# Dilated attention of a prompt: one joint maximum per query, transposed scores in a second pass, and no merge stage

## The chip, the cores and the metric

The kernel runs on one core of one Trainium2 chip. It is one launch: a 2,048-token prompt and 64 new tokens of eight samples go through one layer of a hybrid decoder. The metric is the device time of the launch in microseconds; lower is better.

## What is computed

The layer has three mixers side by side. The change concerns mixer B for the prompt, six heads of width 64, with three branches that share queries, keys and values: each query sees its own token and earlier ones at distance up to 128 (dilation 1), up to 512 (dilation 4), and up to 2,048 (dilation 16). Each branch is a softmax attention of its own; the branches are then merged with their softmax denominators:

```python
for window, dil in DILATIONS:            # ((128, 1), (512, 4), (2048, 16))
    s = einsum('bnirhe,bnjrhe->bnrhij', qs, kk) * scale    # blocks of 128 queries, 256 keys
    s = where(valid, s, -inf)
    mx = max(s, axis=-1);  p = exp(s - mx);  den = sum(p, axis=-1)
    outs.append(einsum('bnrhij,bnjrhe->bnirhe', p, vv) / den)
    lses.append(mx + log(den))
w = softmax(stack(lses), axis=0)
y_b = einsum('gbth,gbthe->bthe', w, stack(outs))
```

Taken together this is sum(p v) / sum(p) over all keys of all branches, with any common shift in the exponent. The projections before (`w_in`) and the output projection and the MLP behind are matrix products of the whole token set.

## The kernel before

The program is a chain of stages. Each has its own tiles and semaphores, and a barrier of all engines stands between two of them (`Mem.clear`, L70). Inside a stage every engine's instruction order is written out by hand, with semaphore waits between engines.

`project_phase` (L90) multiplies 17 tiles of 128 tokens by `w_in` in three passes over column ranges. TensorE (PE) does three matmuls per product; ScalarE (ACT) evicts each of the three column blocks of a tile (L295); SyncE (SP) stores them. `turns` lists the column groups that TensorE also transposes (L353), so that queries and keys lie with the head dimension on partitions in the scratch tensor `qkT`. In the third pass, which makes mixer B's queries, keys and values, only the last tile (the samples) is turned; the rows go to the scratch tensor `nat`.

`stick_prompt_phase` (L385) is mixer C. It matters here because it holds the matmuls that are nearest to the new ones: L584 does the scores of two heads with a 64-row contraction each, one in the upper and one in the lower half of the array.

`dilated_prompt_phase` (L628) handles 48 units: 16 blocks of 128 queries in each of the three branches. For one unit SP loads 128 rows of q, k and v of all heads from `nat` (L735). PE transposes q and k (L846), DVE (VectorE) and ACT copy them out (L791, L755), PE makes the scores of six heads with queries on partitions (L856). DVE adds the mask and takes the maximum in one instruction (L799), ACT takes the exponent with the row sum (L762), PE transposes the exponents (L825), DVE and ACT copy these (L781, L751), PE multiplies them with the values (L836), DVE evicts (L785), and GpSimd (POOL) stores output, maximum and sum to the scratch tensor `br` (L725).

`dilated_merge_phase` (L867) loads the three branches' rows for 128 tokens (L908), makes the weights on DVE in a row of small dependent instructions (L949 to L957), scales and adds (L958 to L961), transposes on PE (L977) and stores. The mLSTM stage follows, then the samples' stages, the output projection and the MLP.

## Time and profile before

| | |
|---|---|
| time, median of 3 runs | 4319.52 us (4317.83 to 4326.96) |
| the profiled execution | 4320.33 us, its span 4318.9 us |
| busy over the span | PE 3868.3 us (90%), DVE 1814.8 (42%), ACT 1410.2 (33%), POOL 1010.1 (23%) |
| projections | 0 to 704.8 us |
| mixer C, prompt | 704.8 to 1313.2 us |
| dilated attention, prompt | 1313.2 to 1675.3 us |
| merge | 1675.3 to 1783.3 us |
| all that follows | 1783.3 us to the end |

The stages don't overlap, because of the barriers. So the span is the sum of the stages, and each stage has its own bound: the busy shares over the whole span say nothing about one of them. The times of the stages are read where the first instruction of a stage starts. The busy time of PE is modelled for each matmul with its drain, so 100% doesn't mean that the array streams all the time.

### The profile page before, as it was taken

The numbers are of one execution on the slowest core, as the hardware profiler recorded it, in microseconds if no ns is written. First come the engines' busy times: TensorE is split into PE (matmuls) and PEld (weight loads), VectorE is DVE, ScalarE is ACT, GpSimd is POOL, SyncE is SP. The second block draws the span as 40 slices with busy tenths as digits, with TensorE's granted clock in tenths as the row PEclk, the third lists the DMA queues.
The fourth block names the chain that finished last, engine by engine and source line by source line (L and its number), as shares of the span: only waits on it lengthen the run. The fifth ranks groups of instructions, "written<-read, shape, count | busy, mean of one in ns | idle before, by whom it ended". The sixth has DMA issues, their size and how long they took to land. (4 is left out here: it accounts for less than half of the span.)

```text
span 4318.9 us, 62472 instructions
## 1 busy us (share of the span) xinstructions
PE 3868.3 (90%) x22579; PEld 3248.4 (75%) x22579; DVE 1814.8 (42%) x3743; ACT 1410.2 (33%) x3007; POOL 1010.1 (23%) x1192
## 2 busy tenths in 40 slices
PE   6999998999998984383669979799999999999998
PEld 6999996343437873383446658699999999999998
DVE  2211002555555666554236654443343443433533
ACT  2311113666664452120224532223223223222222
POOL 2111002444441000131124520051150240330310
PEclk9999998999999997555779989899999999999999
DMA  4654443010002333321939955545555546546433
GB/s 167 220 179 166 163 162 118 6 35 6 8 3 86 103 118 113 95 75 43 256 125 369 362 180 173 170 129 166 181 166 177 180 141 209 160 153 216 136 117 110
DMA packets 457305, 619.63 MB, mean 143 GB/s; under 512 B 43701, under 2 KB 352566, under 8 KB 454230
## 3 DMA queue, kind: packets, MB, share of 16 engines
q1 hardware_dynamic: 415406, 481.52, 35.2%
q0 software_dynamic: 24064, 75.82, 5.0%
q10 hardware_dynamic: 17578, 58.81, 4.1%
q8 instruction: 168, 2.75, 0.3%
q14 instruction: 89, 0.73, 0.1%
HBM read 508.96 MB, written 157.20 MB: 154 GB/s over the span
## 5 line engine op out<-in xcount | busy, mean ns | idle before, releaser
L3049 PE MATMUL p_PS<-p_HI,p_WUH 128*128 128x424 f32 (+1 forms) x1280 | 457.7, 358 | 16.1 <-DVE p_WUL L2985 16.1
L3051 PE MATMUL p_PS<-p_HI,p_WUL 128*128 128x424 f32 (+1 forms) x1280 | 455.0, 355 | 0.0
L3050 PE MATMUL p_PS<-p_LO,p_WUH 128*128 128x424 f32 (+1 forms) x1280 | 453.4, 354 | 0.0
L3050 PE MATMUL p_PS<-p_UL,p_WDH 128*128 128x424 f32 (+1 forms) x1280 | 452.9, 354 | 0.0
L3049 PE MATMUL p_PS<-p_UH,p_WDH 128*128 128x424 f32 (+1 forms) x1280 | 452.7, 354 | 0.0
L3051 PE MATMUL p_PS<-p_UH,p_WDL 128*128 128x424 f32 (+1 forms) x1280 | 452.4, 353 | 0.0
L374 PE MATMUL p_PP<-p_WH,p_HH 128*128 128x384 f32 (+1 forms) x1224 | 414.1, 338 | 27.3 <-DVE p_WL L305 27.3
L2995 DVE TENSOR_TENSOR p_WDL<-p_WD,p_WDH 128x512 fp32r<-128x512 f32 x320 | 221.2, 694 | 455.0 <-ACT p_WDH L2928 455.0
L375 PE MATMUL p_PP<-p_WL,p_HH 128*128 128x384 f32 (+1 forms) x1224 | 406.8, 332 | 0.0
L376 PE MATMUL p_PP<-p_WH,p_HL 128*128 128x384 f32 (+1 forms) x1224 | 406.5, 332 | 0.0
L2873 POOL CAST p_WUH<-p_WU 128x1024 fp32r<-128x1024 f32 x160 | 168.7, 1054 | 931.6 <-PE p_PS L3051 535.4
L2928 ACT ACTIVATE p_WDH<-p_WD 128x512 fp32r<-128x512 f32 x320 | 201.1, 631 | 488.2 <-PE p_PS L3051 480.4
L2985 DVE TENSOR_TENSOR p_WUL<-p_WU,p_WUH 128x1024 fp32r<-128x1024 f32 x160 | 211.4, 1323 | 325.9 <-POOL p_WUH L2873 325.9
L464 POOL TENSOR_TENSOR pc_SL<-pc_SL,pc_L 128x512 f32<-128x512 f32 (+3 forms) x216 | 232.1, 1090 | 200.8 <-DVE pc_L L548 200.8
L295 ACT ACTIVATE p_PT<-p_PP,p_rs 128x384 f32<-128x384 f32 (+1 forms) x153 | 87.2, 570 | 549.6 <-PE p_PP L376 549.6
L2919 ACT ACTIVATE p_R<-p_PS 128x424 f32<-128x424 f32 (+1 forms) x160 | 83.8, 524 | 547.3 <-PE p_PS L3051 547.3
L3049 PEld LDWEIGHTS p_PS<-p_HI,p_WUH 128*128 128x128 f32 x1280 | 241.2, 188 | 21.5 <-issue 16.5
L374 PEld LDWEIGHTS p_PP<-p_WH,p_HH 128*128 128x128 f32 x1224 | 231.5, 189 | 30.7 <-DVE p_WL L305 23.7
L3051 PEld LDWEIGHTS p_PS<-p_HI,p_WUL 128*128 128x128 f32 x1280 | 241.2, 188 | 7.5
L3050 PEld LDWEIGHTS p_PS<-p_LO,p_WUH 128*128 128x128 f32 x1280 | 241.4, 189 | 6.0
L3049 PEld LDWEIGHTS p_PS<-p_UH,p_WDH 128*128 128x128 f32 x1280 | 240.6, 188 | 5.2
L3051 PEld LDWEIGHTS p_PS<-p_UH,p_WDL 128*128 128x128 f32 x1280 | 240.5, 188 | 5.2
(427 smaller groups left out, 7223.6 us busy)
## 6 DMA issues: line engine op xcount, KB each, us to landing
p_WU<-in_w_up SPq DMA_DIRECT2D x160, 512.0 KB, 4.1
p_WD<-in_w_down SPq DMA_DIRECT2D x320, 256.0 KB, 2.7
sc_KP<-in_cache_sb_k SPq DMA_DIRECT2D x256, 192.0 KB, 5.3
sc_VP<-in_cache_sb_v POOLq DMA_DIRECT2D x256, 192.0 KB, 5.7
pb_X<-scratch_nat SPq DMA_DIRECT2D x48, 576.0 KB, 3.6
out_s_wk<-in_cache_win_k ACTq DMA_DIRECT2D x64, 382.5 KB
out_s_wv<-in_cache_win_v ACTq DMA_DIRECT2D x64, 382.5 KB
p_HH<-scratch_xh SPq DMA_DIRECT2D x34, 512.0 KB, 4.5
```

Of the source, the lines that this page charges most:

```text
L295: act.activation(PT[v % 2][:, a - o:e - o], PP[(3 * v + b) % 4][:, 0:e - a], ACT.Copy, scale=rs[:, t:t + 1]).then_inc(blk_ok, 1)
L374: pe.matmul(out, HH[s][:, k, :], wh, start=(k == 0), stop=False)
L375: pe.matmul(out, HH[s][:, k, :], wl, start=False, stop=False)
L376: ins = pe.matmul(out, HL[s][:, k, :], wh, start=False, stop=(k == KD - 1))
L464: ins = pool.tensor_tensor(new[:, a:CH], old[:, a:CH], L[u % 4][:, a:CH], ALU.add)
L2873: pool.tensor_copy(WUH[u % RU][:, :, :], WU[u % RU][:, :, :]).then_inc(wh_ok, 1)
L2928: act.activation(WDH[g % RS][:, :], WD[:, g % RD, :], ACT.Copy).then_inc(dh_ok, 1)
L2985: dve.tensor_tensor(WUL[u % RU][:, :, :], WU[u % RU][:, :, :], WUH[u % RU][:, :, :].bitcast(F32), ALU.subtract).then_inc(wl_ok, 1)
L2995: dve.tensor_tensor(WDL[g % RS][:, :], WD[:, g % RD, :], WDH[g % RS][:, :].bitcast(F32), ALU.subtract).then_inc(dl_ok, 1)
L3049: pe.matmul(out, hi, rhi, start=first, stop=False)
L3050: pe.matmul(out, hi, rlo, start=False, stop=False)
L3051: return pe.matmul(out, lo, rhi, start=False, stop=last)
```

## The change

Four things are changed.

1. In the third pass of the projections all 17 tiles are turned, not only the last. The stores of the same columns to `nat` are gone; the samples' stage reads its new values from the output tensor `s_wv` instead.
2. The dilated stage is rewritten, head by head. A pair is two units of one branch; a head has 24 pairs, six heads 144. A first pass (`natural` on PE, `maximum` on DVE) makes scores with queries on partitions and keeps only the row maxima. The maxima of the three branches are brought into one order through the scratch tensor `bm` (SP's `maxima` and `spread`), DVE's `joint` takes the largest, and SP loads it back, spread over all partitions (`MB`). A second pass (`scores`) makes the same scores again with keys on partitions; DVE subtracts the joint maximum of each query (`shifted`), ACT takes the exponent (`weights`), POOL zeroes what the band leaves out (`select`), and PE multiplies with a tile of 64 value columns and 64 columns of ones (`values`), so that 64 rows of the result hold the sum of the exponents. All branches accumulate in four PSUM banks; the third branch has another order of the tokens and is copied out first (`branch3`, `total`). The division is a logarithm and an exponent on ACT and a product on POOL. The first pass runs 36 pairs ahead of the second, the values three pairs behind it.
3. Queries, keys and values are loaded whole, one head at a time; both halves of the partitions hold the same head, so that the two units of a pair can use the two halves of the array.
4. The merge stage is gone.

In the code `b` is the branch, 0 for dilation 1, 1 for dilation 4, 2 for dilation 16; `u` is one of its 16 blocks. Tokens of branch 1 stand 16 bytes apart in `Q`, `K` and `MB`, tokens of branch 2 64 bytes.

```diff
@@ project_phase
-            return [(0, 0, 3, GB), (1, NB, 3, GB + 3)] if t == NT else []
+            return [(0, 0, 3, GB), (1, NB, 3, GB + 3)]
...
-                if p == 2:
-                    sp.dma_start(S["nat"][rows, QB:QC], part(QB, QC)).then_inc(p_out[s], 16)
@@ dilated_prompt_phase, whole body replaced
+    CY, NU, LEAD, LAG, NE = 24, 48, 36, 3, 6
+    TOTAL = HB * CY
+    TILE, HALF = SEQ // P, P // 2
+    def pair(j):
+        j = j % CY
+        if j < 8:
+            return 2, (2 * j, 2 * j + 1)
+        if j < 16:
+            n = (j - 8) // 2 * 4 + (j - 8) % 2
+            return 0, (n, n + 2)
+        return 1, (2 * (j - 16), 2 * (j - 16) + 1)
+    def ahead(a):
+        return pair(a + 8)
+    def width(b, u):
+        return P if b == 2 or u == TILE - 1 and b == 0 or b == 1 and u >= TILE - 4 else 2 * P
+    def earlier(b, u):
+        return b == 0 and u > 0 or b == 1 and u >= 4
+    def tokens(x, b, u, first, n):
+        if b == 0:
+            return x[:, (u + first) * P:(u + first + n) * P]
+        if b == 1:
+            lo = (u // 4 + first) * P
+            return x.rearrange("p (m f) -> p f m", f=4)[:, u % 4, lo:lo + n * P]
+        return x.rearrange("p (m f) -> p f m", f=16)[:, u, :]
...
+        MB = [m.sb(f"MB{i}", [P, SEQ]) for i in range(2)]
...
+        AC = [m.ps(f"AC{i}", [P, 512]) for i in range(4)]
+        ST = m.ps("ST", [P, 2, 512])
+        SA = m.ps("SA", [P, 2, 512])
...
+            def load_qk(h):
+                g, d, i = h // 2, slice(h % 2 * HD, (h % 2 + 1) * HD), h % 3
+                if h >= 3:
+                    sp.wait_ge(st_ok, upto(h - 3, CY - 1))
+                for dst, src in ((Q[i], S["qkT"][GB + g]), (K[i], S["qkT"][GB + 3 + g])):
+                    for a in range(2):
+                        sp.dma_start(dst[a * HD:(a + 1) * HD, :], src[d, 0:SEQ]).then_inc(qk_in[i], 16)
+            def load_v(h):
+                if h >= 2:
+                    sp.wait_ge(pv_ok, upto(h - 2, CY - 1))
+                v = O["p_wv"][:, h * HD:(h + 1) * HD]
+                for b, rows in ((2, v.rearrange("(i f) c -> i f c", f=16)), (0, v.rearrange("(n i) c -> i n c", i=P))):
+                    sp.dma_start(VV[h % 2][:, b * TILE:(b + 1) * TILE, h % 2, :], rows).then_inc(v_in[h % 2], 16)
+                for n in range(4):
+                    rows = v[n * 512:(n + 1) * 512, :].rearrange("(i f) c -> i f c", f=4)
+                    sp.dma_start(VV[h % 2][:, TILE + 4 * n:TILE + 4 * n + 4, h % 2, :], rows).then_inc(v_in[h % 2], 16)
+            def maxima(h):
+                s = h % 2
+                sp.wait_ge(mx_ok, 2 * upto(h, 15))
+                with nc.allow_non_contiguous_dma(reason="one maximum each"):
+                    sp.dma_start(S["bm"][h, 0, :].rearrange("(n i) -> i n", i=P), MX[s][:, 0, :]).then_inc(m_out[s], 16)
+                for n in range(4):
+                    sp.dma_start(S["bm"][h, 1, n * 512:(n + 1) * 512].rearrange("(i f) -> i f", f=4),
+                                 MX[s][:, 1, 4 * n:4 * n + 4]).then_inc(m_out[s], 16)
+                sp.wait_ge(m_out[s], 16 * 5 * (h // 2 + 1))
+                if h >= 2:
+                    sp.wait_ge(mj_ok, h - 1)
+                sp.dma_start(MR[s][:, :, :], S["bm"][h, 0:2, :].rearrange("b (p f) -> p b f", f=TILE)).then_inc(r_in[s], 16)
+            def spread(h):
+                s = h % 2
+                sp.wait_ge(mj_ok, h + 1)
+                sp.dma_start(S["bm"][h, 2, :].rearrange("(p f) -> p f", f=TILE), MJ[s][:, :]).then_inc(j_out[s], 16)
+                sp.wait_ge(j_out[s], 16 * (h // 2 + 1))
+                if h >= 2:
+                    sp.wait_ge(sub_ok, upto(h - 2, CY - 1))
+                sp.dma_start(MB[s][:, :], row_bcast(S["bm"][h, 2, :], P)).then_inc(mb_in[s], 16)
...
+            load_qk(0)
+            load_qk(1)
+            load_v(0)
+            load_qk(2)
+            load_v(1)
+            for h in range(HB):
+                if h >= 2:
+                    load_v(h)
+                maxima(h)
+                spread(h)
+                if h >= 1 and h + 2 < HB:
+                    load_qk(h + 2)
+                if h >= 2:
+                    store(h - 2)
+            store(HB - 2)
+            store(HB - 1)
...
+            def select(j):
+                b, us = pair(j)
+                x = EX[j % NE]
+                pool.wait_ge(e_ok, j + 1)
+                ins = pool.affine_select(out=x[:, :, 0:P], in_=x[:, :, 0:P], compare_op=ALU.is_ge, fill=0.0, base=0,
+                                         pattern=[[0, 2], [1, P]], channel_multiplier=-1)
+                n = sum(width(b, u) == 2 * P for u in us)
+                if n:
+                    ins = pool.affine_select(out=x[:, 0:n, P:], in_=x[:, 0:n, P:], compare_op=ALU.is_ge, fill=0.0, base=0,
+                                             pattern=[[0, n], [-1, P]], channel_multiplier=1)
+                ins.then_inc(sel_ok, 1)
+            def output(h, k, selected):
+                c = slice(k * 512, (k + 1) * 512)
+                pool.wait_ge(rd_ok, 4 * h + k + 1)
+                if h >= 2 and k == 0:
+                    pool.wait_ge(y_out[h % 2], 16 * (h // 2))
+                pool.wait_ge(sel_ok, selected)
+                pool.tensor_tensor(YT[h % 2][kept(h), c], FN[kept(h), c], RD[kept(h), c], ALU.mult).then_inc(y_ok, 1)
+                pool.wait_ge(y_ok, 4 * h + k + 1)
...
+            def inverse(h, k):
+                c = slice(k * 512, (k + 1) * 512)
+                act.wait_ge(fn_ok, 4 * h + k + 1)
+                if h:
+                    act.wait_ge(y_ok, 4 * (h - 1) + k + 1)
+                act.activation(RD[kept(h), c], FN[summed(h), c], ACT.Ln).then_inc(ln_ok, 1)
+                act.wait_ge(ln_ok, 4 * h + k + 1)
+                act.activation(RD[kept(h), c], RD[kept(h), c], ACT.Exp, scale=-1.0).then_inc(rd_ok, 1)
...
+            def maximum(a):
+                h, (b, us) = a // CY, ahead(a)
+                s = h % 2
+                if a % CY == 0 and h >= 2:
+                    dve.wait_ge(m_out[s], 16 * 5 * (h // 2))
+                dve.wait_ge(sa_ok, a + 1)
+                for i, u in enumerate(us):
+                    c = slice(0 if earlier(b, u) else P, 2 * P)
+                    dve.tensor_tensor_reduce(out=junk[i][:, c], in0=SA[:, i, c], in1=mask[:, c], scale=1.0, scalar=-3e38,
+                                             op0=ALU.add, op1=ALU.max, accum_out=MX[s][:, b, u:u + 1]).then_inc(mx_ok, 1)
+            def joint(h):
+                s = h % 2
+                dve.wait_ge(r_in[s], 16 * (h // 2 + 1))
+                dve.wait_ge(mx_ok, 2 * upto(h, CY - 1))
+                dve.tensor_tensor(MR[s][:, 0, :], MR[s][:, 0, :], MR[s][:, 1, :], ALU.max).then_inc(ja_ok, 1)
+                dve.wait_ge(ja_ok, h + 1)
+                if h >= 2:
+                    dve.wait_ge(j_out[s], 16 * (h // 2))
+                dve.tensor_tensor(MJ[s][:, :], MR[s][:, 0, :], MX[s][:, 2, :], ALU.max).then_inc(mj_ok, 1)
+            def shifted(j):
+                h, (b, us) = j // CY, pair(j)
+                x = EX[j % NE]
+                if j % CY == 0:
+                    dve.wait_ge(mb_in[h % 2], 16 * (h // 2 + 1))
+                dve.wait_ge(st_ok, j + 1)
+                if j >= NE:
+                    dve.wait_ge(pv_ok, j + 1 - NE)
+                w = [width(b, u) for u in us]
+                if w[0] == w[1]:
+                    ins = dve.tensor_tensor(x[:, :, 0:w[0]], ST[:, :, 0:w[0]], both(MB[h % 2], b, us, w[0]), ALU.subtract)
+                else:
+                    for i, u in enumerate(us):
+                        ins = dve.tensor_tensor(x[:, i, 0:w[i]], ST[:, i, 0:w[i]], tokens(MB[h % 2], b, u, 0, w[i] // P), ALU.subtract)
+                ins.then_inc(sub_ok, 1)
+            def total(h, k):
+                dve.wait_ge(pv_ok, upto(h, 17 + 2 * k))
+                dve.wait_ge(b3_ok, 4 * h + 4)
+                if h and k == 0:
+                    dve.wait_ge(y_ok, 4 * h)
+                dve.tensor_tensor(FN[:, k * 512:(k + 1) * 512].rearrange("p (i f) -> p i f", f=16),
+                                  AC[k][:, :].rearrange("p (i f) -> p i f", f=16),
+                                  B3[:, :].rearrange("p (f i) -> p i f", f=16)[:, 32 * k:32 * k + 32, :], ALU.add).then_inc(fn_ok, 1)
+            for a in range(LEAD):
+                maximum(a)
+                if a == CY + 4:
+                    joint(0)
+            for j in range(TOTAL):
+                if j + LEAD < TOTAL:
+                    maximum(j + LEAD)
+                shifted(j)
+                h, i = divmod(j, CY)
+                if i == CY - (LEAD - CY) and h + 1 < HB:
+                    joint(h + 1)
+                done = j - LAG - 2
+                if done >= 0 and done % CY in (17, 19, 21, 23):
+                    total(done // CY, (done % CY - 17) // 2)
...
+            def rows(i):
+                return slice(i * HALF, (i + 1) * HALF)
+            def natural(a):
+                h, (b, us) = a // CY, ahead(a)
+                if a % CY == 0:
+                    pe.wait_ge(qk_in[h % 3], 64 * (h // 3 + 1))
+                if a:
+                    pe.wait_ge(mx_ok, 2 * a)
+                for i, u in enumerate(us):
+                    n = 2 if earlier(b, u) else 1
+                    ins = pe.matmul(SA[:, i, (2 - n) * P:2 * P], tokens(Q[h % 3][rows(i), :], b, u, 0, 1),
+                                    tokens(K[h % 3][rows(i), :], b, u, 1 - n, n), start=True, stop=True)
+                ins.then_inc(sa_ok, 1)
+            def scores(j):
+                h, (b, us) = j // CY, pair(j)
+                if j:
+                    pe.wait_ge(sub_ok, j)
+                for i, u in enumerate(us):
+                    w = width(b, u)
+                    ins = pe.matmul(ST[:, i, 0:w], tokens(K[h % 3][rows(i), :], b, u, 0, 1),
+                                    tokens(Q[h % 3][rows(i), :], b, u, 0, w // P), start=True, stop=True)
+                ins.then_inc(st_ok, 1)
+            def values(j):
+                h, (b, us) = j // CY, pair(j)
+                if j % CY == 0:
+                    pe.wait_ge(v_in[h % 2], 16 * 6 * (h // 2 + 1))
+                if h and j % CY in (0, 2, 4, 6):
+                    pe.wait_ge(fn_ok, 4 * (h - 1) + j % CY // 2 + 1)
+                pe.wait_ge(sel_ok, j + 1)
+                for i, u in enumerate(us):
+                    for bank, lo, w in pieces(b, u):
+                        if b == 0:
+                            pe.wait_ge(b3_ok, 4 * h + bank + 1)
+                        ins = pe.matmul(column(AC[bank], b, u, bank, w), VV[h % 2][:, b * TILE + u, :, :].rearrange("p a e -> p (a e)"),
+                                        EX[j % NE][:, i, lo:lo + w], start=opened[(b == 2, bank)] == (b, u), stop=True, skip_group_check=True)
+                ins.then_inc(pv_ok, 1)
+            pe.wait_ge(ones_ok, 1)
+            for a in range(LEAD):
+                natural(a)
+            for j in range(TOTAL):
+                scores(j)
+                if j + LEAD < TOTAL:
+                    natural(j + LEAD)
+                if j >= LAG:
+                    values(j - LAG)
+            for j in range(TOTAL - LAG, TOTAL):
+                values(j)
@@ dilated_sample_phase
-            act.dma_start(VN[:, :, :], S["nat"][SEQ:SEQ + NS, VB:QC].rearrange("(b t) c -> t b c", t=DT)).then_inc(ok["new_in"], 16)
+            act.dma_start(VN[:, :, :], O["s_wv"][:, WIN - DT:WIN, :].rearrange("b t c -> t b c")).then_inc(ok["new_in"], 16)
@@ build
-        ("br", (3, SEQ, NB + 2 * HB)),
+        ("bm", (HB, 3, SEQ)),
...
-    dilated_merge_phase(nc, A, S, O)
```

On PE, in the dilated stage before, one unit of the first two branches (`pb_SP` holds scores, then turned exponents, then outputs; `pb_TP` the turned queries and keys):

```order
L856 MATMUL pb_SP<-pb_KT,pb_QT 128x128 x12
L836 MATMUL pb_SP<-pb_X,pb_PT 128x64 x12
L846 MATMUL pb_TP<-pb_ident,pb_X 128x128 x6
L822 ISA
L825 MATMUL pb_SP<-pb_ident,pb_PR 128x128 x4
L822 REGISTER_ALU
```

and after the change, two pairs in the middle of a head (`pb_ST` the scores of the second pass, `pb_SA` those of the first, `pb_AC` the accumulators):

```order
L1002 MATMUL pb_ST<-pb_Q,pb_K 128x256 x2
L992 MATMUL pb_SA<-pb_K,pb_Q 128x256 x2
L1017 MATMUL pb_AC<-pb_EX,pb_VV 128x256
L1017 MATMUL pb_AC<-pb_EX,pb_VV 128x128
L1002 MATMUL pb_ST<-pb_Q,pb_K 128x256 x2
```

Two more groups of four such transposes follow before. The transposes are gone from the stage; scores of a pair of units of one head alternate with the first-pass scores of the pair 36 further on.

On DVE, one unit before (the L799 pairs come three times):

```order
L785 COPY pb_OT<-pb_SP 128x384
L788 REGISTER_ALU
L791 COPY pb_KT<-pb_TP 64x384 x2
L780 ISA
L781 COPY pb_PT<-pb_SP 128x1024
L799 ISA pb_SM,pb_OT<-pb_SP,pb_mask 128x256
L799 ISA pb_OT 128x1
L799 ISA pb_SM,pb_OT<-pb_SP,pb_mask 128x256
```

and after:

```order
L923 ISA pb_junk,pb_MX<-pb_SA,pb_mask 128x256
L923 ISA pb_MX 128x1
L923 ISA pb_junk,pb_MX<-pb_SA,pb_mask 128x256
L923 ISA pb_MX 128x1
L946 TENSOR_TENSOR pb_EX<-pb_ST,pb_MB 128x512
L923 ISA pb_junk,pb_MX<-pb_SA,pb_mask 128x256
```

The copies are gone. In each pair DVE first takes two maxima (those of the pair 36 ahead) and then subtracts, and the next pair's maxima come behind that.

## Rows read from the trace of the kernel before

**Rows 1.** Stretches of stages (us, busy and instructions per engine, PEclk, DMA share, GB/s)

```profile
704.82:1313.24 608.42, 595.83 (x2064) 242.84 (x2064) 319.19 (x495) 384.87 (x721) 272.87 (x320) 0.99 0.06 21
1313.24:1675.30 362.06, 311.80 (x2538) 283.09 (x2538) 234.71 (x920) 171.55 (x673) 27.40 (x53) 0.97 0.32 106
1675.30:1783.26 107.96, 14.38 (x48) 8.05 (x48) 69.98 (x192) 3.49 (x17) 0.49 (x3) 0.50 0.45 119
```

**Rows 2.** Waits of the dilated stage: engine line, waited for, us, times, longest

```profile
ACT pb_PR L762 <- DVE pb_nm L805: 174.2, 49, 5.8
```

**Rows 3.** Timeline of ACT in the projections' second pass: start us, us

```profile
454.10 0.58 ACT L295 ACTIVATE p_PT<-p_PP,p_rs 128x384 f32<-128x384 f32 x1 [3.93 <-PE p_PP L376]
458.67 0.58 ACT L295 ACTIVATE p_PT<-p_PP,p_rs 128x384 f32<-128x384 f32 x1 [3.98 <-PE p_PP L376]
462.77 0.58 ACT L295 ACTIVATE p_PT<-p_PP,p_rs 128x384 f32<-128x384 f32 x1 [3.52 <-PE p_PP L376]
467.26 0.58 ACT L295 ACTIVATE p_PT<-p_PP,p_rs 128x384 f32<-128x384 f32 x1 [3.91 <-PE p_PP L376]
```

**Rows 4.** Timeline of mixer C: 64-row score matmuls of two heads, full clock

```profile
726.90 0.49 PE L584 MATMUL pc_ZP<-pc_QS,pc_K 64*128 64x128 f32 x4
727.32 0.71 PE L587 MATMUL pc_ZP<-pc_mask,pc_ident 128*128 128x128 f32 x4
...
731.77 0.70 PE L584 MATMUL pc_ZP<-pc_QS,pc_K 64*128 64x256 f32 x4
732.40 0.38 PE L587 MATMUL pc_ZP<-pc_mask,pc_ident 128*128 128x128 f32 x1
```

**Rows 5.** The same timeline, from a score matmul to the DVE instruction behind it

```profile
999.86 1.13 PE L584 MATMUL pc_ZP<-pc_QS,pc_K 64*128 64x512 f32 x4
...
1001.04 0.75 DVE L539 TENSOR_SCALAR pc_E<-pc_ZP,pc_bsb 128x512 f32<-128x512 f32 x1 [1.66 <-PE pc_ZP L584]
```

**Rows 6.** Timeline of the dilated stage: mask and maximum, 256 and 128 keys

```profile
1403.98 0.42 DVE L799 CUSTOM_DVE_ANT_0 pb_SM<-pb_SP,pb_mask 128x256 f32<-128x256 f32 x1 [1.74 <-PE pb_SP L856]
...
1404.33 0.42 DVE L799 CUSTOM_DVE_ANT_0 pb_SM<-pb_SP,pb_mask 128x256 f32<-128x256 f32 x1
...
1595.70 0.29 DVE L799 CUSTOM_DVE_ANT_0 pb_SM<-pb_SP,pb_mask 128x128 f32<-128x128 f32 x1 [2.23 <-POOLq L727]
...
1595.92 0.29 DVE L799 CUSTOM_DVE_ANT_0 pb_SM<-pb_SP,pb_mask 128x128 f32<-128x128 f32 x1
```

**Rows 7.** Groups by shape, mixer C: a DVE instruction on PSUM and SBUF

```profile
L548 DVE SCALAR_TENSOR_TENSOR pc_L<-pc_ZP,pc_bsb,pc_E 128x512 f32<-128x512 f32 x168 | 126.2, 751 | 94.9 <-ACT pc_E L493 94.9
```

**Rows 8.** Timeline of the dilated stage: from a DVE instruction to the waiting PE

```profile
1663.86 0.69 DVE L781 COPY pb_PT<-pb_SP 128x512 f32<-128x512 f32 x1 [1.10 <-PE pb_SP L825]
...
1664.70 0.29 PE L836 MATMUL pb_SP<-pb_X,pb_PT 128*128 128x64 f32 x1 [0.87 <-DVE pb_PT L781]
```

**Rows 9.** Timeline of PE in the dilated stage: twelve full-array matmuls of 128 columns

```profile
1400.82 2.84 PE L856 MATMUL pb_SP<-pb_KT,pb_QT 128*128 128x128 f32 x24
1403.49 0.33 PE L836 MATMUL pb_SP<-pb_X,pb_PT 128*128 128x64 f32 x2
```

**Rows 10.** Timeline of POOL in the dilated stage

```profile
1313.92 0.29 POOL L715 TENSOR_SCALAR_AFFINE_SELECT pb_ident<-pb_ident 128x128 f32<-128x128 f32 x1
```

**Rows 11.** Timeline of mixer C's start: first matmul, and two groups at the low clock

```profile
713.58 0.80 PE L584 MATMUL pc_ZP<-pc_QS,pc_K 64*128 64x128 f32 x4 [20.01 <-DMA pc_K<-scratch_qkT]
...
715.46 1.23 PE L584 MATMUL pc_ZP<-pc_QS,pc_K 64*128 64x256 f32 x4
```

**Rows 12.** Stretches (as Rows 1): third branch of the dilated stage, and the mLSTM stage

```profile
1630.00:1645.00 15.00, 12.37 (x95) 10.06 (x93) 10.29 (x54) 7.76 (x37) 1.08 (x2) 1.00 0.36 112
1800.00:1960.00 160.00, 140.04 (x658) 129.48 (x659) 83.76 (x262) 44.99 (x138) 46.51 (x75) 0.50 0.22 65
```

**Rows 13.** Groups by shape, mixer C: POOL and ACT on 512 columns

```profile
L464 POOL TENSOR_TENSOR pc_SL<-pc_SL,pc_L 128x512 f32<-128x512 f32 x144 | 179.9, 1271 | 200.8 <-DVE pc_L L548 200.8
...
L491 ACT ACTIVATE pc_E<-pc_E 128x512 f32<-128x512 f32 x168 | 104.4, 621 | 138.3 <-DVE pc_E L539 138.3
```

More of the change, by code:

```diff
@@ L149, in stores @@
         def stores(p, t):
-            a = [1, 2, 3][p]
-            return a + (2 * DB - 2 if p == 2 and t == NT else 0)
+            return 2 * DB if p == 2 and t == NT else [1, 2, 2][p]
         def stored(p, t):
@@ L663, in each @@
-    def each(eng, step):
-        for trips, first, prev, rows, before in bodies:
-            if trips == 1:
-                for q in range(4):
-                    step(first + q, q, prev[q], lambda v, q=q: rows(v, 0, q), prev[q - 1] if q else before)
-                continue
-            with eng.Fori(0, trips) as i:
-                for q in range(4):
-                    step(i * 4 + (first + q), q, prev[q], lambda v, q=q: rows(v, i, q), prev[q - 1] if q else before)
+    CY, NU, LEAD, LAG, NE = 24, 48, 36, 3, 6
@@ new lines, in pieces, with column @@
+    def pieces(b, u):
+        if b == 2:
+            return [(u // 4, 0, P)]
+        if b == 0:
+            if width(b, u) == P:
+                return [(u // 4, 0, P)]
+            return [(u // 4, 0, 2 * P)] if u % 4 < 3 else [(u // 4, 0, P), (u // 4 + 1, P, P)]
+        return [(u // 4 + i, i * P, P) for i in range(width(b, u) // P)]
+    def column(acc, b, u, bank, w):
+        if b == 2:
+            return acc[:, u % 4 * P:u % 4 * P + P]
+        if b == 1:
+            return acc.rearrange("p (m f) -> p f m", f=4)[:, u % 4, :]
+        lo = max(u * P - bank * 512, 0)
+        return acc[:, lo:lo + w]
@@ L729, in _ @@
-            each(pool, step)
-        @block.sync
-        def _(sp):
-            def step(u, q, prev, rows, before):
-                wait_apart(sp, pv_ok, u + 2, passed)
-                sp.dma_start(X[q][:, :, :, :].rearrange("p a g c -> p (a g c)"), rows(views)).then_inc(x_in[q], 16)
-            each(sp, step)
+            for h in range(2):
+                ins = pool.memset(VV[h][:, :, 1 - h, :], 1.0)
+            ins.then_inc(ones_ok, 1)
+            def select(j):
+                b, us = pair(j)
+                x = EX[j % NE]
[7 more added lines that the diff above has]
+                ins.then_inc(sel_ok, 1)
@@ L740, in _ @@
+            for k in range(4):
+                output(HB - 1, k, TOTAL)
         @block.scalar
@@ L829, in values @@
-            def values(u, q, prev):
-                n = 2 if prev else 1
-                pe.wait_ge(pa_ok, u + 1)
-                pe.wait_ge(pb_ok, u + 1)
-                for h in range(HB):
-                    for k in range(n):
-                        slot = (q - 1) % 4 if n == 2 and k == 0 else q
-                        ins = pe.matmul(SP[q % 2][:, 0, h * HD:(h + 1) * HD], PT[q % 2][:, h // 2, (h % 2) * n + k, :],
-                                        X[slot][:, 2, h // 2, h % 2 * HD:(h % 2 + 1) * HD], start=(k == 0), stop=(k == n - 1))
-                ins.then_inc(pv_ok, 1)
```

348 lines of the change are left out of this document (97 added, 251 removed).

## The prediction

> **What bounds the stages that change.** I read the stretches first. Barriers separate the stages, so only the edited ones matter: the dilated stage takes 362.1 us and the merge 108.0, 470.0 together; in the first PE is busy 86% at a granted clock of 0.97, in the merge only DVE has work, 70 of 108 us, and that in short dependent steps [rows 1]. The waits of the dilated stage show a loop from DVE's maxima over ACT to PE's transposes: ACT waited 174.2 us for the negated maximum [rows 2]. So before, PE is near its bound in one stage, and latency rules the other. The new stage has to be priced as a loop too, since each engine waits for another in every pair.
>
> **The projections.** 16 more tiles are turned, six transposes each. In the second pass, which turns the same way, the three column blocks of a tile end 4.57, 4.10 and 4.49 us apart, the 4.10 without a turn [rows 3]. A turn of six costs 13.16 - 3 x 4.10 = 0.86 us, on PE, which is the bound there. 16 x 0.86 = **+14 us**. The store to `nat` gives way to the smaller one to `qkT`, on a queue and DMA engines that PE doesn't wait for in this pass: nothing. The samples' new values come from another tensor in one load: nothing.
>
> **The new loop.** `ST` and `SA` are single tiles. PE may write `ST` for a pair only after DVE has subtracted the pair before; behind that on PE stand the first-pass scores into `SA`; DVE takes the two maxima of `SA` before it subtracts. So one pair costs, in a row: scores, first-pass scores, two maxima, subtraction, and two handovers. The value matmuls, ACT and POOL lie beside it.
>
> A full pair (2 x 256 columns in both passes):
> - scores: two 64-row matmuls in two halves of the array, start to the next group's start, 732.40 - 731.77 = 0.63 us [rows 4];
> - first-pass scores up to DVE's start: modelled end 0.70 [rows 4] plus 0.05 (999.86 + 1.13 to 1001.04) [rows 5]: 0.75;
> - two maxima, each 0.35 after the one before: 0.70 [rows 6];
> - subtraction, 512 elements, PSUM and SBUF in: 0.751 by the nearest instruction [rows 7], 0.69 by a plain eviction [rows 8]; I take 0.72;
> - DVE's end to PE's start, 1663.86 + 0.69 to 1664.70: 0.15 [rows 8].
>
> Sum **2.95 us**. A short pair (2 x 128): 0.42 + (0.49 + 0.05) [rows 4, 5] + 2 x 0.22 [rows 6] + 0.42 for 256 elements, as a maximum takes [rows 6] + 0.15 = **1.97 us**. A head has, counted from `width` and `earlier`, 14 full and 10 short pairs (one mixed pair counted as full) in either pass: 14 x 2.95 + 10 x 1.97 = 61.0, six heads **366 us**.
>
> What comes on top:
> - The first 36 maxima run alone, and so do the last 36 subtractions: 36 more handovers each way, 36 x 0.27 = 10 us.
> - The clock. After the loads PE starts at 1.2 GHz, where the same groups have modelled ends of 0.80 and 1.23 instead of 0.49 and 0.70 [rows 4, 11]: +0.31 short, +0.53 full. In the lead of 36 (24 full, 12 short) PE waits for DVE's maxima in every pair, so I keep it at the low clock: 24 x 0.53 + 12 x 0.31 = 16. The first 12 pairs of the loop, mostly short, likely too: 10 more. 26 us.
> - Second waits in front of instructions and the mixed pairs' split subtraction: estimate 4 us, from 0 to 12.
> - Start: 713.58 - 704.82 = 8.8 us from a stage's start to its first matmul behind a load of 2 MB [rows 1, 11]; head 0's queries and keys are 2 MB too: 9 us.
> - End: four inversions of two ACT steps, below 0.62 each, one product below 1.27 on POOL [rows 13], a store and the barrier: 13 us.
>
> Sum 366 + 10 + 26 + 4 + 9 + 13 = **428 us** for the 470 removed: **-42**. With the projections **-28 us**.
>
> What I cost at nothing, and its cover:
> - Value matmuls: 128 columns over the full array take (1403.49 - 1400.82)/12 = 0.22 [rows 9], a full pair's four 0.89 us. They have from the end of the first-pass scores to the next pair's start, 0.12 + 0.70 + 0.72 + 0.15 = 1.7 us. In the last 36 pairs the slack is 0.2 us.
> - POOL's zeroing: 0.29 for 128 elements [rows 10], so some 0.5 for 256, two per full pair: 1.0 of 2.95 us. If it takes over 0.87 each it becomes the bound of the last 36.
> - The trip of the maxima through memory (five stores, a load, a store, a spread load of 1 MB): for later heads nine pairs, some 20 us, lie between store and `joint`, and 12 more before the first subtraction. For head 0 the stores queue on SP's queue behind 9 MB of loads, 3 MB of these in pieces of 256 bytes. The maxima of its first 16 pairs are there after about 43 us, `joint` is reached at about 72, the lead ends at 89. I expect no wait; if the loads take over 60 us, each us beyond costs one.
>
> **Strided reads.** Two of the three branches read `Q`, `K` and `MB` with steps of 16 and 64 bytes, which no large operand does in this trace, so no row prices them; bounds are nothing and twice the streaming. I take nothing, since an fp32 matmul takes 1.7 ns per column [rows 9], which leaves a reader time. The Trainium skill says otherwise (SBUF — State Buffer, SBUF: two separate sides, in its note on cachelines): a read needs two hits in each 16-byte line for full rate. By it the sum gains rival 2's amount. No row here can show it.
>
> **Rivals.**
> 1. *The clock stays low.* The mLSTM stage has PE 88% busy by the modelled ends and still runs at 0.50 throughout, while the third branch of the old stage is 82% busy and stays at 1.00 [rows 12]. So neither level is safe from the busy share. In the new loop at the low clock a full pair is 4.01 us, and the scores and the values fill it without a gap, like nothing in the mLSTM stage; that speaks for a rise. If it never rises: 84 x 1.06 + 60 x 0.62 = 126 instead of the 26, and the value matmuls, 1.8 us, no longer fit: +8. Time 4292 + 108 = **4400 us**. If it only falls again in each head's short pairs, some 8 us a head: **4336 us**.
> 2. *Strided reads cost, and the kernel is slower.* In the 16 pairs of a head of branches 1 and 2, 10 are short and 6 full. If streaming doubles, both passes gain 2 x (6 x 0.43 + 10 x 0.21) = 9.4 us, the subtraction 6 x 0.5 + 10 x 0.25 = 5.5: 15 us a head, 89 us. Time **4381 us**. It decides from a third of that penalty on, since 28 us are to be lost.
> 3. *The clock is high throughout*, the lead too, because DVE and PE alternate quickly: 26 us less, **4266 us**. Against it: in the lead PE waits for DVE in every pair, and the stage starts at the low clock [rows 11].
>
> **How the numbers follow.** The sum goes against the profiled execution, 4320.3 us, 0.8 above the median of the runs: 4320.3 - 28 = **4292 us**. Chances: forecast 0.47 (its own range 4276 to 4310), rival 3 0.10, clock falling in short pairs 0.11, strided reads 0.20 (4335 to 4390), clock low throughout 0.12. The range 4262 to 4388 takes in all but the last of these. A measurement of this kernel can tell some 0.2%, 9 us, from no change. Faster by more: 0.60; within: 0.08; slower: 0.32.
>
> **What the new profile would show.** The dilated stage starts 14 us later than 1313.2 and lasts 428; full pairs 2.9 to 3.0 us apart on the subtraction's line, short ones 2.0; DVE idle about 1.4 us per full pair, waiting for PE; the clock 0.5 for the first 100 us and 1.0 then; no wait of DVE for a load beyond a few us. I am wrong if a pair of branch 1 takes longer than one of branch 0 (strides), if POOL's selects end the values' wait and PE's scores are behind them, or if the last 36 pairs, priced at 1.8 us full, take over 2.

## The result, and the profile after

| | before | after |
|---|---|---|
| median of the runs | 4324.69 us (15 runs) | 4331.26 us (4328.24 to 4336.68, 15 runs) |
| ratio to before | | 1.0017, 95% interval 1.0009 to 1.0024 |
| span of the profiled execution | 4318.9 us | 4330.7 us |

The changed kernel is slower by 0.17%. The interval doesn't take in a ratio of 1, but the difference lies inside the 0.2% that I called "no change"; I had forecast 28 us less. So 35 us are to be explained. (The two profiled executions lie 11.8 us apart, the medians 6.6; the stages below add up to the former.) The four stretches of the profile after, by the first instruction of each stage (columns: window, its length, busy time of each engine with its count of instructions, the granted clock of PE, share of the DMA engines, GB/s):

```profile
0.00:715.33 715.33, 672.29 (x4080) 665.61 (x4080) 108.00 (x160) 130.88 (x240) 75.27 (x32) 0.99 0.49 163
715.33:1323.06 607.73, 595.17 (x2064) 242.62 (x2064) 319.00 (x495) 384.89 (x721) 272.79 (x320) 0.99 0.06 21
1323.06:1794.01 470.95, 373.36 (x1908) 252.47 (x1908) 216.69 (x762) 120.48 (x223) 124.36 (x257) 0.81 0.32 68
1794.01:4330.70 2536.69, 2286.44 (x13945) 2059.42 (x13945) 1099.66 (x2008) 719.36 (x1357) 633.47 (x785) 0.92 0.55 172
```

Against [rows 1], the projections are 10.5 us longer, mixer C is 0.7 shorter, and all that follows is 1.1 longer. The new dilated stage lasts 471.0 us, where I had forecast 428. It replaces 470.0 us and gains nothing. The same view splits it into the lead (up to the first subtraction), the loop of 108 pairs with both passes, and the last 36 pairs:

```profile
1323.06:1405.67 82.61, 41.40 (x152) 20.02 (x152) 25.47 (x151) 1.28 (x1) 6.05 (x5) 0.50 0.62 128
1405.67:1713.90 308.23, 264.43 (x1401) 187.24 (x1402) 155.04 (x566) 87.20 (x164) 81.91 (x181) 0.85 0.29 61
1713.90:1781.03 67.13, 64.71 (x333) 42.58 (x334) 32.59 (x45) 26.55 (x50) 30.93 (x67) 1.00 0.12 32
```

The end, 1781.03 to 1794.01, is 13.0 us. By my own terms these four would be 77, 286, 52 and 13 us; how each comes out stands in the section on the prediction. The excess is 22 us in the loop, 15 in the last pairs and 5 in the lead.

The timeline shows one full pair of branch 0 and one of branch 1, both at clock 1.0 and both with the same number of columns in the two passes (start, duration, engine, line, operation). In each, L946 is the subtraction of one pair and, at the end, that of the next; between them stand L1002, the scores of the next pair, L992, the first-pass scores, and L923, the first of the two maxima:

```profile
1509.51 0.69 DVE L946 TENSOR_TENSOR pb_EX<-pb_ST,pb_MB 128x512 f32<-128x512 f32 x1
...
1510.25 0.70 PE L1002 MATMUL pb_ST<-pb_Q,pb_K 64*128 64x256 f32 x4 [0.42 <-DVE pb_EX L946]
...
1510.79 0.60 PE L992 MATMUL pb_SA<-pb_K,pb_Q 64*128 64x256 f32 x4
...
1511.43 0.42 DVE L923 CUSTOM_DVE_ANT_0 pb_junk<-pb_SA,pb_mask 128x256 f32<-128x256 f32 x1 [1.24 <-PE pb_SA L992]
...
1512.12 0.69 DVE L946 TENSOR_TENSOR pb_EX<-pb_ST,pb_MB 128x512 f32<-128x512 f32 x1
```

```profile
1521.43 1.05 DVE L946 TENSOR_TENSOR pb_EX<-pb_ST,pb_MB 128x512 f32<-128x512 f32 x1
...
1522.53 1.28 PE L1002 MATMUL pb_ST<-pb_Q,pb_K 64*128 64x256 f32 x4 [0.78 <-DVE pb_EX L946]
...
1523.63 0.61 PE L992 MATMUL pb_SA<-pb_K,pb_Q 64*128 64x256 f32 x4
...
1524.29 0.42 DVE L923 CUSTOM_DVE_ANT_0 pb_junk<-pb_SA,pb_mask 128x256 f32<-128x256 f32 x1 [1.82 <-PE pb_SA L992]
...
1524.98 1.04 DVE L946 TENSOR_TENSOR pb_EX<-pb_ST,pb_MB 128x512 f32<-128x512 f32 x1
```

In branch 1, where MB, Q and K are read with a step of 16 bytes, the subtraction takes 1.05 us instead of 0.69 and the scores 1.28 instead of 0.70. The first-pass scores of that pair belong to branch 0 (the passes are 36 pairs apart) and cost no more. From subtraction to subtraction that is 3.55 us; in branch 0 it is 2.61 here, and 2.62 in nearly all pairs of the loop that are full and of branch 0 in both passes. This is the sign I had named for rival 2, the strided reads.

At the low clock the strides cost the matrix engine next to nothing. Two full pairs of the lead, of branch 0 and of branch 1:

```profile
1343.98 1.23 PE L992 MATMUL pb_SA<-pb_K,pb_Q 64*128 64x256 f32 x4 [0.88 <-DVE pb_MX L923]
```

```profile
1361.78 1.28 PE L992 MATMUL pb_SA<-pb_K,pb_Q 64*128 64x256 f32 x4 [0.88 <-DVE pb_MX L923]
```

So in the loop the strides took away what the high clock gives. The view by windows of two equal steps with strides in both passes (second pass of branch 2, first pass of branch 1), one at the high clock and one at the low, has the same length for both, 3.09 us:

```profile
1551.22:1554.31 3.09, 2.36 (x12) 1.50 (x12) 2.27 (x7) 0.42 (x1) 0.41 (x1) 1.00 0.80 242
1620.89:1623.98 3.09, 2.87 (x14) 1.92 (x13) 2.27 (x9) 0.42 (x1) 0.41 (x1) 0.50 0.64 202
```

### The profile page after: what moved, and what is told of

It reads as the page before. It is cut to its first block and busy times, and to the rows that moved or that the text cites. A ratio compares the mean times of both kernels' runs of the same rounds, so it can differ in the third digit from the quotient of the medians.

```text
span 4330.7 us, 59154 instructions
## 1 busy us (share of the span) xinstructions
PE 3927.3 (91%) x21997; PEld 3220.1 (74%) x21997; DVE 1743.3 (40%) x3425; ACT 1355.6 (31%) x2541; POOL 1105.9 (26%) x1394
```

## The experiments

Each is an edit of the changed kernel unless it says otherwise. e1, e2, e3, e5, e10 and e11 leave out the dilation of branches 1 and 2 in the operands named, so these branches attend to wrong tokens or subtract wrong maxima; they price the strides and are no kernels to use. The others leave nothing out. Times are medians; the ratio is to the kernel before, run beside it, with its 95% interval.

| label | edit | us | ratio (interval) |
|---|---|---|---|
| e1_contiguous | Q, K, MB read in blocks | 4270.6 | 0.9882 (0.9863 to 0.9902) |
| e2_contiguous_mb | MB alone | 4309.9 | 0.9974 (0.9965 to 0.9984) |
| e3_contiguous_qk | Q and K alone | 4284.8 | 0.9913 (0.9895 to 0.9931) |
| e5_contiguous_stationary | the stationary operand alone | 4319.0 | 0.9996 (0.9987 to 1.0005) |
| e6_before_turned | before, with the turned tiles | 4333.2 | 1.0024 (1.0014 to 1.0033) |
| e4_subtract_first | DVE subtracts first | 4285.6 | 0.9921 (0.9904 to 0.9938) |
| e7_maxima_before_values | e4, maxima stored first | 4271.5 | 0.9883 (0.9868 to 0.9899) |
| e9_maxima_first_alone | maxima stored first, alone | 4330.0 | 1.0012 (1.0003 to 1.0022) |
| e10_contiguous_maxima_first | e1, maxima stored first | 4250.3 | 0.9828 (0.9812 to 0.9844) |
| e11_contiguous_both_orders | e10 with e4 | 4213.3 | 0.9746 (0.9730 to 0.9763) |
| e8_three_orders_of_maximum | e7, MB in three orders | 4342.6 | 1.0049 (1.0034 to 1.0065) |
| e12_lead_30 | e7, lead of 30 pairs | 4256.8 | 0.9838 (0.9821 to 0.9856) |

### Strides taken away: e1, e2, e3, e5

```diff
-            return x.rearrange("p (m f) -> p f m", f=4)[:, u % 4, lo:lo + n * P]
-        return x.rearrange("p (m f) -> p f m", f=16)[:, u, :]
+            return x.rearrange("p (f m) -> p f m", f=4)[:, u % 4, lo:lo + n * P]
+        return x.rearrange("p (f m) -> p f m", f=16)[:, u, :]
```

This is `tokens` (Q and K, e3); the same in `both` (MB) is e2, and e1 has the two. e5 has it only where `tokens` gives the stationary operand.

> The changed kernel, but branches 1 and 2 read Q, K and MB in contiguous blocks of 128 or 256 columns in place of every 4th or 16th element; numbers, shapes and order of the instructions are the same. So these two branches attend to wrong tokens: the kernel leaves out the dilation. Theory (the strides are what the new stage lost): in the loop a pair of branch 1 takes 3.56 us and one of branch 0 2.62 with the same columns. With contiguous reads both should take 2.6, a short pair beside a full one 2.15 in place of 3.09, short beside short 1.7 to 2.35 (by the clock), the subtraction of branch 1 0.69 in place of 1.05. That is some 16 us a head over the 4.5 heads of the loop and 15 in the last 36 pairs: 4331 - 87 = 4244 us, up to 4290 if PE, less busy, gets the low clock for longer. Rival (the clock and the chain of handovers are what was lost, strides cost nothing): the steps stay as they are, within 10 us of 4331.

> Only MB, the joint maximum that DVE subtracts, is read in contiguous blocks for branches 1 and 2 (so wrong maxima are subtracted there); Q and K are read with strides. Theory: the subtraction falls from 1.05 to 0.69 in full pairs of branch 1 (36 of them) and from 0.58 to 0.42 in the short ones (60 and more), all of it on the loop: 36 x 0.36 + 66 x 0.16 = 23 us, 4308 us. Rival (DVE's part is hidden by PE's): the step of a pair stays, 4331.

> Only Q and K are read in contiguous blocks (so branches 1 and 2 attend to wrong tokens); MB is read with strides. Theory: the matmuls' part of the loss is the rest, 87 - 23 = 64 us: 4267 us; a full pair of branch 1 takes 3.0 in place of 3.56, two short pairs 1.9. Rival (the matrix engine takes 1.7 ns per fp32 column anyway, and a strided read keeps up): no change, 4331.

> As the run with contiguous Q and K, but only the stationary operand of the score matmuls (the one that is loaded as weights) is read in contiguous blocks; the moving one and MB are read with strides (so branches 1 and 2 attend to wrong tokens). Theory (the moving operand costs, weight loads overlap with it): a weight load of 64 rows takes 0.31 us with stride and 0.19 without; at most one load in each of 192 strided groups shows, so 5 to 15 us: 4320 us (4314 to 4327), of the 46 us that Q and K cost together. Rival (the stationary operand is half of it): 4308.

e1 is 61 us faster than the changed kernel (4331.3 to 4270.6), so the rival "clock and handovers" falls: the order of work and the handovers were not touched. The clock wasn't held, its falls in the loop became shorter; but a strided step lasts 3.09 us at either level, so the clock alone gives no such gain. MB alone gives 21 us (23 expected), Q and K 46 (64 expected), the stationary operand 12 of these (its ratio has an interval of some 4 us on either side). So the larger part of Q and K's cost, 34 us and more, is left with the moving operand. The steps of a full pair of branch 1 beside one of branch 0, in which no wait for memory falls, say the same: 3.56 us in the changed kernel, 3.43 in e5, 3.20 in e2, 2.98 in e3, and 2.62 in e1, as in branch 0. e1 and e3 stayed 27 and 18 us short of the theory's number, and the view of the tile `MR` in e1 says where it went, in a wait that the changed kernel doesn't have:

```profile
L930 DVE TENSOR_TENSOR pb_MR<-pb_MR x6: 163/174/177, 1390.6 to 1665.1; 128x16 f32<-128x16 f32 x6
...
  DMA pb_MR<-scratch_bm: 17.5, 4
```

Four of the six `joint` steps now wait for the maxima's trip through memory, 17.5 us in all, and everything on DVE is queued behind `joint`. The pairs had become faster than the trip.

### The new wait taken away: e9, e10

```diff
-                if h >= 2:
-                    load_v(h)
                 maxima(h)
+                if h >= 2:
+                    load_v(h)
```

> The changed kernel with the reordering of SP's queue alone: a head's maxima are stored ahead of the load of its values, DVE's order as it was. Theory (in the changed kernel joint never waits, since the slow pairs leave the stores time enough; the wait appears only when the pairs get faster): no change, 4331 (4327 to 4335). Rival (the load of values holds up something else in the changed kernel too): 5 us or more less.

> As e1 (branches 1 and 2 read contiguous blocks, so they attend to wrong tokens), with the maxima's stores ahead of the load of values. Theory (e1 lost some of its gain to a new wait: joint waited 17.5 us for the maxima, and POOL's outputs bunched behind it): 18 to 25 us less than e1's 4270.6: 4250 us, so that the strides cost 80 us and not 61. Rival (the joint wait was hidden by PE's work): e1's 4270.

Alone the edit changes nothing that can be told (4330.0 against 4331.3), as expected, since the changed kernel has no such wait. On top of e1 it gives 20 us, 4250.3. So **the strides cost 81 us** (4331.3 - 4250.3; 80 against e9, which differs from e10 in the strides alone), of which e1 hid a quarter. The stage of e10 lasts 388.1 us by the same window view, and its loop shows what my sum should have given without strides, a clock of 1.0 nearly throughout among it:

```profile
1405.10:1645.30 240.20, 198.63 (x1401) 143.51 (x1402) 137.90 (x567) 87.07 (x164) 81.95 (x181) 0.97 0.34 73
```

### The projections: e6

In the kernel before, `turns` gives the column groups of the third pass for every tile (the store to `nat` stays):

```diff
-            return [(0, 0, 3, GB), (1, NB, 3, GB + 3)] if t == NT else []
+            return [(0, 0, 3, GB), (1, NB, 3, GB + 3)]
```

> The kernel before with one part of the change alone: all 17 tiles of the third pass are turned and stored to qkT; the store to nat stays too, since the old dilated stage reads it. Theory (16 turns of 0.66 us each, as the profile of the changed kernel shows with its stage 10.5 us longer): 10.5 us above before, 4335. My prediction's term says 14 us: 4339. Rival (the turns fit into gaps of PE and the 10 us come from elsewhere): within 3 us of before, 4325.

Measured 4333.2 against 4322.8 beside it: +10.4 us, the theory's number. My term of 14 was too high, and the evictions show why. First the third pass of the kernel before, which turns nothing:

```profile
643.01 0.58 ACT L295 ACTIVATE p_PT<-p_PP,p_rs 128x384 f32<-128x384 f32 x1 [3.58 <-PE p_PP L376]
...
655.49 0.58 ACT L295 ACTIVATE p_PT<-p_PP,p_rs 128x384 f32<-128x384 f32 x1 [3.58 <-PE p_PP L376]
```

and of the changed kernel:

```profile
643.91 0.58 ACT L297 ACTIVATE p_PT<-p_PP,p_rs 128x384 f32<-128x384 f32 x1 [3.97 <-PE p_PP L378]
...
657.09 0.58 ACT L297 ACTIVATE p_PT<-p_PP,p_rs 128x384 f32<-128x384 f32 x1 [3.99 <-PE p_PP L378]
```

Three blocks take 12.48 us without a turn and 13.18 with one. The turn is 0.70 us, not 0.86: I had taken all three blocks at the shortest, 4.10.

### The chain of a pair: e4, e7

```diff
-                if j + LEAD < TOTAL:
-                    maximum(j + LEAD)
                 shifted(j)
+                if j + LEAD < TOTAL:
+                    maximum(j + LEAD)
```

> One thing is reordered in the changed kernel: DVE subtracts for pair j before it takes the two maxima of pair j + 36, not behind them. Then PE's next scores and DVE's maxima run at the same time. Theory (a pair is a chain scores, first-pass scores, maxima, subtraction, with each engine waiting for the other): PE's own sequence from scores to the values' end takes 2.18 us in full pairs of branch 0 (step 2.62), 2.56 in branch 1 (3.56), 2.35 for short beside full (3.09), 2.19 at the low clock (2.35); by these the steps fall to PE's sequence, 12 us a head in 4.5 heads: 54 us, 4277 us (4262 to 4300). Rival (PE is the bound already, or the values then wait for POOL's zeroing): 4320 or more.

> Two changes to the changed kernel: the subtraction ahead of the maxima (as in e4), and on SP's queue the stores of a head's maxima ahead of the load of its values (in e4 behind it). Theory (in e4 DVE waits 18.9 us in joint for the maxima, four times some 5 us, because their stores wait behind 1.5 MB of values in pieces of 256 bytes; and POOL's output bunches behind that wait): joint no longer waits, 20 to 25 us less than e4's 4285.6: 4263 us (4258 to 4270). Rival (the maxima's own 4-byte pieces are the delay): 4280 or more.

e4 computes the same and is 46 us faster than the changed kernel: the loop is a chain of handovers, as my prediction's pricing had it, and the order on DVE decides how much of it overlaps. It too ran into `joint`, 18.9 us in four waits. e7 adds the new order on SP's queue and is 14 us faster than e4, 9 less than I expected. Its loop is PE's own sequence now, 243.6 of 247.8 us busy:

```profile
1404.00:1651.80 247.80, 243.62 (x1405) 175.39 (x1405) 157.57 (x570) 87.04 (x164) 82.27 (x180) 0.96 0.32 70
```

The reason I gave for `joint`'s wait was only half right. SP's timeline of a head in e4:

```profile
1474.50 1.73 SPq L787 DMA_DIRECT2D scratch_bm<-pb_MX  x1
1476.27 3.25 SPq L789 DMA_DIRECT2D scratch_bm<-pb_MX  x4
1489.21 0.37 SPq L794 DMA_DIRECT2D pb_MR<-scratch_bm  x1
```

and in e7:

```profile
1470.13 0.38 SPq L787 DMA_DIRECT2D scratch_bm<-pb_MX  x1
1470.55 2.32 SPq L789 DMA_DIRECT2D scratch_bm<-pb_MX  x4
1484.10 0.37 SPq L794 DMA_DIRECT2D pb_MR<-scratch_bm  x1
```

From the last store's issue to the load that waits for the stores it is 9.7 us in e4 and 11.2 in e7. So the values didn't slow the small pieces down; they only let the stores start 4.4 us later. The trip itself is the long part, and the earlier start is what brings it in time. The greater part of the trip is no moving of data: in e7 the stores' last packet starts at 1477.0, and for the 7 us from there to the load the DMA queues show next to nothing. What passes in that time the trace doesn't show.

### Both, and the bound of it: e11

> As e10 and with DVE's subtraction ahead of the maxima: what the stage could be without strides and without the chain (branches 1 and 2 attend to wrong tokens). PE's sequence in a full pair is 2.14 us, short beside full 1.7, short beside short 1.3: 60 x 2.14 or so in a loop of 108 pairs gives 200 us in place of e7's 248, and 8 us go in the last 36 pairs. Theory: 4271 - 48 - 8 = 4216 us. Rival (DVE, or POOL with its selects and outputs, 0.8 and 1.3 us, becomes the bound, or joint is late again): 4230 or more.

Measured 4213.3, the theory's 4216 within 3 us, with the stage at 354.5 us. The strides alone are worth 81 us (e10), the order of the work 60 (e7), both together 118: they overlap by 23 us. That is near the 21 of the subtraction's stride (e2), which the steps of e8 below show hidden behind PE once the work is reordered.

### A cure that made it worse: e8

The joint maximum is stored to `bm` in three orders, loaded as three tiles, and `shifted` reads the one of its branch:

```diff
+                    sp.dma_start(S["bm"][h, 0, :].rearrange("(f p) -> p f", f=TILE), MJ[s][:, :]).then_inc(j_out[s], 16)
+                    for r in range(4):
+                        sp.dma_start(S["bm"][h, 1, r * 512:(r + 1) * 512].rearrange("(p g) -> p g", g=4),
+                                     MJ[s][:, :].rearrange("p (g f) -> p f g", f=4)[:, r, :]).then_inc(j_out[s], 16)
...
+                for b, r in ((2, 0), (0, 2), (1, 1)):
+                    sp.dma_start(MB[s][b][:, :], row_bcast(S["bm"][h, r, :], P)).then_inc(mb_in[s], 16)
```

> On top of e7: the joint maximum is stored in three orders and loaded as three tiles, so that DVE's subtraction reads each branch contiguously; the product is written over RD, and YT is gone, to make room. Nothing is left out. In e2 this alone (with the loop as it was) was worth 21 us. Theory (in e7 PE's sequence bounds the loop and the subtraction is mostly beside it, except in the last 36 pairs, where 3 us go): 3 to 10 us less than e7: 4256 us. Rival (the subtraction is still on the chain of every pair): 20 us less than e7, 4243. Second rival (the two more loads of 1 MB a head and the stores of single elements hold joint or the first subtraction up): above e7.

The second rival came true: 4342.6 us, 71 more than e7. The waits and SP's timeline in e8:

```profile
DVE pb_EX L951 <- DMA pb_MB<-scratch_bm: 73.5, 6, 21.6
```

```profile
1390.03 0.44 SPq L800 DMA_DIRECT2D scratch_bm<-pb_MJ  x1
1390.51 3.00 SPq L802 DMA_DIRECT2D scratch_bm<-pb_MJ  x4
1413.34 1.27 SPq L808 DMA_DIRECT2D pb_MB<-scratch_bm  x3
```

DVE waits for MB in every head, 73.5 us in all. From the issue of the last store in small pieces it is some 20 us (1393.5 to 1413.3) until the load may go, though the view by windows shows the DMA engines idle (share 0.00) from 1402 to 1412, and between `joint` and the next head's first subtraction there are 12 pairs of some 2 us. Where no such wait fell, the steps say that even the gain was not to be had in the loop: a full pair of branch 1 beside one of branch 0 took 2.71 us in e7 and in e8, though the subtraction went from 1.07 to 0.69. In the loop it was hidden behind PE, as the theory of e8 had it.

### The lead: e12

```diff
-    CY, NU, LEAD, LAG, NE = 24, 48, 36, 3, 6
+    CY, NU, LEAD, LAG, NE = 24, 48, 30, 3, 6
...
-                if a == CY + 4:
+                if a == CY + 1:
```

> As e7 (nothing left out), with a lead of 30 pairs in place of 36, joint of head 0 after 26 pairs in place of 29, and joint of the later heads six pairs later in the loop. Theory: a pair alone in the lead takes 2.1 us and one alone in the tail 1.7 to 2.4, together 1.8 more than both in one step of the loop (2.1 to 2.7); six pairs fewer on each side save 8 to 12 us: 4261 us. Rival: between joint and the first subtraction of a head 6 pairs are left, 12 us, for two trips through memory; if they take longer, each us is lost six times: above 4272.

Measured 4256.8: 15 us below e7, more than expected. It leaves nothing out of the computation and **beats both kernels**, 1.6% below before (0.9838, 0.9821 to 0.9856). The trips through memory still fit into the six pairs that are left.

## Why the prediction was wrong

Forecast 4292 us with a range of 4262 to 4388, and 0.60 on faster; it came out at 4331, 7 us slower than before. The step that failed is that the strided reads were costed at nothing: they cost 81 us. That the time still lies inside the range is luck in part, since a second error of 45 us went the other way. Point by point:

- **Projections, +14.** Measured +10.4 (e6). Mechanism right, base for the blocks too low.
- **Start 9, end 13.** The first matmul stood 12.5 us behind the stage's start, 3.5 more; the end took the 13.0 forecast.
- **The lead.** A pair alone at the low clock was to take 0.75 + 0.70 + 0.15 + 0.53 = 2.13 us full and 1.44 short; measured 2.11 and 1.42. 24 and 12 of them are 68 us, 70 measured. With the start, 77 forecast and 82.6 measured. The clock stayed low for the first 109 us of the stage, where I had said 100. The prediction also put `joint` at 72 us and the lead's end at 89, which takes all of its pairs as full; they came at 67 and 82.6, and nothing hung on it.
- **The loop's base, 2.95 us per full pair.** Without strides, and in the changed kernel's own pairs of branch 0 that are full in both passes, it is 2.62. The scores and first-pass scores up to DVE's start took 1.18 us (1510.25 to 1511.43), not 0.63 + 0.75 = 1.38: the second group started 0.54 after the first, not 0.63, and took 0.60, not 0.70. And DVE's end to PE's start took 0.05 (1510.20 to 1510.25), not 0.15. Pairs that are full in one pass alone took 2.14 in e10, where my terms give 2.44 or 2.48. A short pair takes 1.71 in e10, not 1.97. For the 108 pairs with both passes my terms give 60 x 2.80 + 48 x 1.82 + 108 x 0.15 + 14 = 286 us (second and first pass full 1.35 + 1.45, short 0.84 + 0.98, then 10 for the clock and 4 for second waits); e10 took 240.2. So this term was 45 us too high.
- **Strided reads, costed at nothing.** This is the step that failed: the forecast has no term for them, and they cost 81 us (e10), of which 21 by DVE's subtraction (e2). I had bounded them by twice the streaming and took the lower end on the ground that an fp32 matmul takes 1.7 ns per column and "leaves a reader time". It doesn't: 256 columns took 1.28 us with a stride and 0.70 without. The Trainium skill (SBUF — State Buffer, SBUF: two separate sides), which asks for two hits in each 16-byte line, spoke against the change and was right in kind, and the trace agrees with it. It makes no difference between the clock's levels, and the trace does: 1.28 against 1.23 at the low one.
- **The last 36 pairs, 52 us.** Measured 67: full pairs of branch 0 took 1.50 to 1.70, around the 1.62 that my terms give (the 1.8 in the prediction's last paragraph doesn't follow from them), those of branch 1 2.45, and the short ones of branch 2 1.48 instead of 1.11. In e10 the full pairs of both branches took 1.49 to 1.72 and most of branch 2's short ones 1.00 to 1.30. So this excess is strides too, and the sign that I had named, over 2 us for a full pair here, was seen in branch 1.
- **Costed at nothing, and rightly so in the loop:** the value matmuls and POOL's selects (0.41 us each, where I had guessed 0.5; PE's weight loads waited 11.6 us for them in all), and the trip of the maxima, for which `joint` never waited. In the last 36 pairs the value matmuls did cost some 0.2 us per full pair: there the step of branch 0 is 1.50 us where PE has a short pair's values to do and 1.70 where it has a full one's, and PE is busy 64.7 of 67.1 us. The trip's cover was thin: it is the slow pairs that hid the trip, and e1, e3 and e4 lost 13 to 19 us there, and e11 6, as soon as the pairs got faster.
- **Rival 1** (clock low): it fell in the short pairs of four heads, 14 to 17 us each, as that rival said. It cost almost nothing, since strided steps last 3.09 us at either level; only a few pairs of branch 0 that it caught took 2.8 us in place of 2.35. In e10 and e7, with the pairs faster, it did not fall within the loop at all.
- **Rival 2** was the mechanism, with a price of 89 us against 81 measured; I gave it 0.20. Its total of 4381 was 50 too high: 45 in the loop's base, 4 in the projections and 8 in the strides' price were too much, and 3.5 at the start and some 2 each in lead and tail too little.

So two errors of my sum met: 81 us of strides missing, 45 us of chain too many. Together with the smaller terms they leave the 39 us between 4292 and 4331.

## What to carry to other kernels

Before data is read in place with a step of 16 bytes or more by a matmul or by an engine on the critical chain, price the read as if the streaming took 1.5 to 1.8 times as long (measured here for fp32: 0.69 to 1.05 us on DVE, 0.70 to 1.28 on TensorE at the high clock), and look whether the layout can be made contiguous once, where it is written. In a loop in which two engines pass work back and forth, compare orders on the waiting engine first: here two lines swapped were worth 46 us and cost nothing. When a stage gets faster, look again at every trip that was "hidden": list for each how many steps it has, times the new duration of a step.

## What the runs showed of the hardware

- The stride's cost depends on the engine and the clock. PE, 64 rows by 256 columns, fp32: 0.70 to 1.28 us at 2.4 GHz for one group of matmuls, 1.23 to 1.28 at 1.2 GHz. DVE, one of two operands strided in SBUF: 0.69 to 1.05 us for 512 elements, 0.42 to 0.58 for 256, the latter at either level of PE's clock.
- Contiguous stationary operands alone gave 12 us (e5), both operands 46 (e3). The moving operand is the dearer one: with it alone strided the group of scores takes 1.15 us (e5), with both 1.28, with neither 0.70.
- A step of 16 bytes in PSUM on the writing side cost nothing that can be seen: the value matmuls of branch 1 write their columns so, and four of 128 columns take 1.16 us, two of 256 contiguous columns in branch 0 1.13.
- The granted clock fell back to 1.2 GHz inside the loop in two kinds of kernel: for 3 to 7 us in most heads with waits in `joint` (e1, e3, e4, e11), and without such waits where the pairs stayed slow, 14 to 17 us in the changed kernel and e9, 10 to 20 in e5, 3 to 7 in e2. (In e8, with its waits for MB, it fell for up to 27 us.) In e7, e10 and e12, with neither, it stayed at 1.0 from the first pairs of the loop to the last subtraction. So the waits aren't needed for a fall. I have no run that tells what in the slow pairs brings it.
- Stores in pieces of one or a few fp32 elements are slow for their size: five stores with 16 KB in all held up the load behind them by 10 to 11 us, and six with 24 KB by some 20. The one store of 8 KB in pieces of 64 bytes let its load go 1.1 us after its issue (e4, 1491.73 to 1492.82). In both long cases the queues are empty for a good half of the time (7 of 11 us in e7, 13 of 20 in e8), so the packets' own time is the smaller part.

The changed kernel's strided Q and K were not cured, only shown: a version that writes `qkT` in the branches' orders wasn't tried. By e11 against e7, which takes the stride out of MB too, it would have up to 58 us to gain, less what the reordering costs.
